# GpSimd's modulation columns in pairs of 256, multiplied by a scalar per partition

## The reference

```python
shift, scale, gate = jnp.split(s_lat @ w_mod[layer] + b_mod[layer], 3, axis=-1)     # first block
x_in = x * (1.0 + scale[:, None, :]) + shift[:, None, :]
...
shift, scale, gate = jnp.split(c_act @ w_ada[l] + b_ada[l], 3, axis=-1)             # second block
h = rms_norm(x, norm_w[l]) * (1.0 + scale[:, None, :]) + shift[:, None, :]
...
x = x + gate[:, None, :] * y
```

## Time and profile before

| | |
|---|---|
| median of three runs | 2867.41 us (2862.24 to 2875.26) |
| span of the profiled execution | 2862.3 us |
| busy: TensorE, VectorE, ScalarE, GpSimd | 95%, 61%, 42%, 52% |
| mean granted TensorE clock | 0.968 |
| loaded from HBM | 589.46 MB |

### The profile page before, as it was taken

How to read it: one execution, slowest core, us unless ns; L and a number is a source line. 1 busy time by engine, 2 the same in 40 slices (tenths; PEclk the granted TensorE clock), 3 DMA queues, 4 the chain that set the end, 5 groups by cost and what they waited for, 6 DMA issues and landing times.

```text
span 2862.3 us, 51222 instructions
## 1 busy us (share of the span) xinstructions
PE 2705.6 (95%) x22151; PEld 2503.6 (87%) x22151; DVE 1738.4 (61%) x1905; ACT 1209.2 (42%) x1438; POOL 1491.9 (52%) x1071
## 2 busy tenths in 40 slices
PE   5799999999999999999999969999989899999899
PEld 3589999888888899989989959999889899998899
DVE  2344545654555658696677655764866557657763
ACT  1243444333443334344476344633453456334442
POOL 0056766986666788777455604054548440445420
PEclk8699999999999999999999979999999999999999
DMA  9999998998887988777556746755657666656565
GB/s 338 290 306 267 267 267 248 293 283 255 244 234 229 282 252 226 207 218 199 144 160 168 206 102 161 187 152 157 185 145 211 192 162 163 170 148 176 154 170 155
DMA packets 948768, 599.21 MB, mean 209 GB/s; under 512 B 22070, under 2 KB 945088, under 8 KB 948032
## 3 DMA queue, kind: packets, MB, share of 16 engines
q1 hardware_dynamic: 944720, 582.83, 72.8%
q10 hardware_dynamic: 3824, 13.11, 1.2%
HBM read 589.46 MB, written 6.29 MB: 208 GB/s over the span
## 4 chain that ended last, share of the span: by engine, by line
PE 78%; DVE 11%; DMA 6%; ACT 3%; issue 1%; SPq 1%; POOL 0%; DVEq 0%; ACTq 0%; POOLq 0%
PE G L2393 58%; DMA ring<-in_w_mod_dram 3%; DVE ring_r L1466 3%; PE A L2333 2%; DMA const<-in_w_mod_dram 2%; PE A L2453 1%; PE A L2459 1%; PE A L2456 1%; PE G L2475 1%; PE A L2494 1%; ACT ring_r L867 1%; PE A L2638 1%; PE G L2831 1%; SPq L718 1%; DVE M L2169 1%
## 5 line engine op out<-in xcount | busy, mean ns | idle before, releaser
L2393 PE MATMUL G<-H_r,ring_r 128*128 128x256 f32 x10032 | 1700.5, 287 | 52.0 <-DVE S_r L1455 20.7
L2393 PEld LDWEIGHTS G<-H_r,ring_r 128*128 128x128 f32 x10032 | 1473.3, 191 | 84.2 <-issue 56.9
L824 POOL TENSOR_TENSOR ring<-ring,act_in 128x512 f32<-128x512 f32 x448 | 659.9, 1494 | 1159.2 <-DMA ring<-in_w_ada_dram 915.9
L1466 DVE TENSOR_TENSOR ring_r<-ring,ring_r 128x2048 fp32r<-128x2048 f32 x346 | 875.1, 2530 | 274.2 <-ACT ring_r L867 273.2
L867 ACT ACTIVATE ring_r<-ring 128x2048 fp32r<-128x2048 f32 x346 | 661.7, 1912 | 334.4 <-PE G L2393 109.9
L2393 PE MATMUL G<-M_r,ring_r 128*128 128x256 f32 x4528 | 789.5, 284 | 0.0
L2393 PEld LDWEIGHTS G<-M_r,ring_r 128*128 128x128 f32 x4528 | 645.5, 190 | 10.0 <-issue 9.4
L2393 PE MATMUL G<-S_r,ring_r 128*128 128x256 f32 x1920 | 546.5, 285 | 0.0
L827 POOL TENSOR_TENSOR ring<-ring 128x512 f32<-128x512 f32 x224 | 366.5, 1636 | 17.6
L2393 PEld LDWEIGHTS G<-S_r,ring_r 128*128 128x128 f32 x1920 | 369.9, 193 | 3.4 <-issue 3.3
L833 POOL TENSOR_TENSOR ring<-ring 128x256 f32<-128x256 f32 x168 | 211.7, 1260 | 13.2
(11 more groups left out here) (441 smaller groups left out, 2581.8 us busy)
## 6 DMA issues: line engine op xcount, KB each, us to landing
ring<-in_w_in_dram SPq DMA_DIRECT2D x120, 1024.0 KB, 5.7
ring<-in_a_w_in_dram SPq DMA_DIRECT2D x98, 1024.0 KB, 6.8
ring<-in_w_ada_dram SPq DMA_DIRECT2D x192, 512.0 KB, 6.8
const<-in_w_mod_dram SPq DMA_DIRECT2D x192, 256.0 KB, 5.4
ring<-in_c_w_in_dram SPq DMA_DIRECT2D x48, 1024.0 KB, 5.9
ring<-in_w_mod_dram SPq DMA_DIRECT2D x16, 2048.0 KB, 18.0
ring<-in_a_w_out_dram SPq DMA_DIRECT2D x32, 1024.0 KB, 6.4
ring<-in_w_out_dram SPq DMA_DIRECT2D x32, 1024.0 KB, 5.9
```

The source lines that it names most:

```text
L824: g.mark(pool.tensor_tensor(w[:, i:i + 2, :], w[:, i:i + 2, :], act_in[:, k:k + 2, c:c + 1].broadcast_to((P, 2, BW)), ALU.mult))
L1466: v.tensor_tensor(w_low(tl), w_raw(tl), w_up(tl).bitcast(F32), ALU.subtract).then_inc(w_lo, 1)
L2393: ins = pe.matmul(G[tl.bank][:, 0:SEQ], w, x, start=(k == 0 and n_ == 0), stop=(k == KT - 1 and n_ == 2))
```

## The change

A block's four units become a pair of blocks' eight units. A unit is now two row groups by 512 columns (still 512 KB; each run of memory that the load reads is 2 KB long, where it was 1 KB). Both blocks of a pair are multiplied and summed together, in rows of 512 columns. The multiply is a `tensor_scalar` with one input and the activation as a scalar per partition. `mod_rows` has two buffers of 512 columns, one for each pair in turn. The columns of both blocks can be transposed only when the pair's last unit is done, and stand at that tile and the next free one. Beside this `ones` and `mean` are stored as one column and read with a broadcast, and `act_in` is stored three columns a row group instead of 32; TensorE's matmuls with `act_in` read 32 consecutive columns, of which the first three are the ones used, as before.

```diff
-    _q = POOL_TILE[4 * _p + 3] - 1
+    _q = POOL_TILE[8 * (_p // 2) + 7] - 1
...
-        ones = sb("ones", [P, P])
-        mean = sb("mean", [P, P])
-        act_in = sb("act_in", [P, KT, 32])
-        mod_rows = [sb(f"mod_rows{i}", [P, BW]) for i in range(2)]
+        one_col, mean_col = sb("one_col", [P, 1]), sb("mean_col", [P, 1])
+        ones, mean = one_col[:, :].broadcast_to((P, P)), mean_col[:, :].broadcast_to((P, P))
+        act_all = sb("act_in", [P, 3 * KT + 32])
+        act_in = act_all[:, 0:3 * KT].rearrange("p (k i) -> p k i", i=3)
+        mod_rows = [sb(f"mod_rows{i}", [P, 2 * BW]) for i in range(2)]
...
-                l, j = POOL_BLOCKS[m // 4]
-                k = 4 * (m % 4)
+                l, j = POOL_BLOCKS[2 * (m // 8)]
+                k = 2 * (m % 8)
...
-                sp.dma_start(pool_unit(m), mod_w[l][:, k:k + 4, j * BW:(j + 1) * BW]).then_inc(pool_full[m % 2], 16)
+                sp.dma_start(pool_unit(m), mod_w[l][:, k:k + 2, j * BW:(j + 2) * BW]).then_inc(pool_full[m % 2], 16)
...
-                for u in range(4):
-                    m = 4 * p + u
+                for u in range(8):
+                    m = 8 * n + u
...
-                    for i in (0, 2):
-                        k = 4 * u + i
-                        g.mark(pool.tensor_tensor(w[:, i:i + 2, :], w[:, i:i + 2, :],
-                                                  act_in[:, k:k + 2, c:c + 1].broadcast_to((P, 2, BW)), ALU.mult))
+                    for i in range(2):
+                        k = 2 * u + i
+                        g.mark(pool.tensor_scalar(w[:, i, :], w[:, i, :], act_in[:, k, c:c + 1], None, ALU.mult))
                     g.settle()
-                    g(pool.tensor_tensor(w[:, 0:2, :], w[:, 0:2, :], w[:, 2:4, :], ALU.add))
                     if u == 0:
-                        if p >= 2:
-                            pool.wait_ge(pool_cols, p - 1)
+                        if n >= 2:
+                            pool.wait_ge(pool_cols, 2 * n - 2)
...
-                    pe.wait_ge(pool_used, 4 * p + 4)
+                    pe.wait_ge(pool_used, 8 * (p // 2) + 8)
...
-                        ins = pe.transpose(bank[:, t * P:(t + 1) * P], mod_rows[p % 2][:, t * P:(t + 1) * P], ident)
+                        c0 = (p % 2) * BW + t * P
+                        ins = pe.transpose(bank[:, t * P:(t + 1) * P], mod_rows[p // 2 % 2][:, c0:c0 + P], ident)
```

More of the change, by code:

```diff
@@ L502, in pool_unit @@
             at = (RAW + HALF) * KT * P + (m % 2) * 4 * BW
-            return ring[:, at:at + 4 * BW].rearrange("p (k c) -> p k c", c=BW)
+            return ring[:, at:at + 4 * BW].rearrange("p (k c) -> p k c", c=2 * BW)
         late = [(CONST_AT["rot128"][0], CONST_AT["keep"][0] + SEQ),
@@ L810, in _ @@
             g = Signals(pool, g_own)
-            for what, value in ((ones[:, :], 1.0), (mean[:, :], 1.0 / D), (act_in[:, :, :], 0.0)):
+            for what, value in ((one_col[:, :], 1.0), (mean_col[:, :], 1.0 / D), (act_all[:, :], 0.0)):
                 g.mark(pool.memset(what, value))
@@ L893, in _ @@
                     act.wait_ge(first_cols, b - 1)
-                act.activation(mod_rows[b % 2][:, :], G[2 * (b % 2)][:, 0:BW], ACT.Copy).then_inc(first_rows, 1)
+                act.activation(mod_rows[b % 2][:, 0:BW], G[2 * (b % 2)][:, 0:BW], ACT.Copy).then_inc(first_rows, 1)
                 if b % 2 and b >= 3:
@@ L2424, in mla @@
                 for j in range(4):
-                    ins = pe.matmul(A[0][:, 0:SEQ], ones[:, :], rms_sq[j], start=(j == 0), stop=(j == 3))
+                    ins = pe.matmul(A[0][:, 0:SEQ], ones, rms_sq[j], start=(j == 0), stop=(j == 3))
                 PS.done(ins, "kvsum")
@@ L2434, in mla @@
                     for j in range(4):
-                        ins = pe.matmul(A[2][:, t:t + 1], rms_sq[j][:, t * P:(t + 1) * P], ones[:, 0:1],
+                        ins = pe.matmul(A[2][:, t:t + 1], rms_sq[j][:, t * P:(t + 1) * P], one_col[:, :],
                                         start=(j == 0), stop=(j == 3))
@@ L2537, in four_sums @@
                 for g in range(4):
-                    ins = pe.matmul(bank[32 * g:32 * g + 32, 0:SEQ], mean[:, 0:32], four[:, g, :], start=first, stop=last,
+                    ins = pe.matmul(bank[32 * g:32 * g + 32, 0:SEQ], mean_col[:, :].broadcast_to((P, 32)), four[:, g, :], start=first, stop=last,
                                     skip_group_check=True)
@@ L2549, in last_sums @@
                     together(bank, part, True, False)
-                return pe.matmul(bank[:, SEQ:2 * SEQ], mean[:, :], x, start=False, stop=(n == KT - 1), skip_group_check=True)
+                return pe.matmul(bank[:, SEQ:2 * SEQ], mean, x, start=False, stop=(n == KT - 1), skip_group_check=True)
             product("ac_out", HR256, HR2, quarters("ac_out"), Pace(sums(0, "ac_out", XH, A[0])))
@@ L2605, in gqa @@
                                 ins = pe.matmul(A[3][:, BW + 4 * t + r:BW + 4 * t + r + 1],
-                                                sq_q1[g % 2][:, r, t * P:(t + 1) * P], ones[:, 0:1], start=True, stop=True)
+                                                sq_q1[g % 2][:, r, t * P:(t + 1) * P], one_col[:, :], start=True, stop=True)
                         PS.done(ins, f"qsum{g}")
@@ L2714, in mixers @@
                                   start=True, stop=True)
-                    pe.matmul(A[2][:, 0:2], ones[:, :], small[:, 50:52], start=True, stop=True)
+                    pe.matmul(A[2][:, 0:2], ones, small[:, 50:52], start=True, stop=True)
                     for p in range(2):
```

10 lines of the change are left out of this document (5 added, 5 removed).

## The result

The changed kernel takes 2842.47 us (median of 4 runs, 2835.71 to 2847.17) against 2864.82 us for the kernel before in 4 runs (2861.77 to 2875.26). The ratio is 0.991, 95% interval 0.9888 to 0.9932. The kernel became faster by about 22 to 26 us (the difference of the medians and the ratio), twice what I forecast, and mostly not by the steps that I forecast.

What follows compares the result with a forecast made beforehand. TensorE, busy 2705.6 of 2862.3 us, was taken as the bound. The terms -3.5 - 7 - 2 + 1.5 = -11 us took the span from 2862.3 to 2851.3 and the median from 2867.4 to 2856.4; 8-in-10 range 2841 to 2876.

Steps and rivals of the forecast that it cites:

- signs I had named: Checks: GpSimd busy near 1190 us; TensorE waiting for VectorE before L2356, or SP for GpSimd above 98.6 us, would refute.
- The duration of the multiply by a scalar: On GpSimd, 512 columns: taken as 0.65 us, near the memset's 0.530, bounded above by 2.1.
- B: VectorE's full stretches: fewer GpSimd pieces block VectorE, and one block's columns leave each norm; -7 us (0 to -15).
- four stretches: From 1100, 1200, 2055 and 2630 us, VectorE nearly full beside GpSimd; TensorE idle 22.1 us together.
- 19 us of waiting in the norms: Two norms, 16 L1672 each, every one losing 0.62 us while GpSimd works.
- only the adds would block, and B would be near -14: If VectorE were free beside one-input instructions, only the adds, 19.4 of 37.5 us, would block it.
- A: SP's 12.6 us hold ending at 2130.37, behind GpSimd's wait for a transpose, goes; -3.5 us (0 to -6).
- C: Stretches at the DMA's limit, 540 to 620 us: longer load runs help a little; -2 us (0 to -6).
- D: Neighbouring transposes: TensorE's second transpose of a pair waits for VectorE's reading of the first; +1.5 us (0 to +6).
- Narrow tensors: Broadcast and 32-column window change only the addresses weight loads read, not the matmuls or columns; 0 us.
- the cheap instruction: Rival, 20%: the one-input multiply takes 0.53 us and VectorE often gets in before GpSimd; -22 us, 2845 us.
- The slow instruction that holds SP: Rival, 10%: from 540 to 620 a slow multiply holds SP's queue and TensorE waits for weights; 2886 us at 1.6 us.

Runs made afterwards that it cites:

- pair_tt: The changed kernel with the two-input multiply of before in place of the multiply by a scalar; 2869.46 us, ratio 1.0018 to the kernel before.
- four_rows: The kernel before with the narrow tensors and four row buffers of 256 columns instead of two; 2858.6 us, ratio 0.9973.
- runs_1k: The changed kernel with each GpSimd unit loaded as two DMAs of 1 KB runs; 2844.5 us, ratio 0.9927 to the kernel before.
- single_ts: The kernel before with narrow tensors and four multiplies by a scalar of 256 columns in each old unit, without pairs; 2906.11 us, ratio 1.0149.
- ports2: Small kernel without the layers' computation, GpSimd and VectorE instructions alone and together; VectorE's 256-column `tensor_scalar` is `a`, 1024-column `tensor_tensor` `b`; memset 524 ns.

## Why the prediction was wrong

The range held the time by 1.5 us (2841 to 2876), and the forecast of -11 us was half of what came. That it came so near is luck: an instruction much slower than I took was priced by a wrong rule, and the two errors went opposite ways. Of the signs I had named, three came against me: GpSimd is busy 1644.8 us and not near 1190, SP waits 113.7 us for it and not below 98.6, and TensorE waits 0.9 us for VectorE before L2356. The steps, one by one.

**The duration of the multiply by a scalar.** Taken 0.65 us, measured 1.57. I bounded it from 0.53 to 2.1 and went to the memset as the nearest row, because one input is less than two. It was the wrong neighbour: the number of inputs does not set the time by itself (a copy, also with one input, takes 614 ns). The scalar column is not what costs, since a multiply by an immediate takes 1490. The Trainium skill (GPSIMD Engine Reference, "When to use GPSIMD") has one-input operations at roughly line rate, from which my estimate was 0.53 to 0.6 us; the trace disagrees with 1.57.

**B, the failed step.** "Only the number of pieces falls": I priced the blocking of VectorE by the mean length of GpSimd's instructions and their number, and held a one-input instruction to block like any other. `pair_tt` has the fewer pieces and loses 5 us; the changed kernel has instructions half as long again and gains 22 to 26. What counts is the form: 0.7 to 0.95 us lost by a scale-and-shift that meets a two-input instruction, 0.2 us beside the multiply by a scalar. From 1.0018 to 0.991 this is 31 us, with an error of 8; less the 7 us that the pair as a unit costs it is 24, against 7 taken and 15 as the far end. The far end was too near because I took it as two thirds of the idle time in four stretches. The 6 us near 1600, the largest single step, lie in none of them: there TensorE waited 5.1 us for VectorE in the kernel before (`PE G L2393 <- DVE X L1685`), and I had left that stretch out of the sum. How the rest is spread over smaller waits is not resolved. The rule of the Trainium skill (SBUF — State Buffer, "SBUF: two separate sides"), on which I leaned, has the pair held exclusively for the whole instruction. By it an `a` beside the 1566 ns multiply would take 1.5 to 1.6 us, an estimate with the two thirds to three quarters of the other's length that it loses beside the two-input ones. It takes 620 ns, so the measurement decides against it for this pair of instructions; for two-input ones the runs are near it. My 19 us of waiting in the norms were a slip, 32 x 0.616 is 19.7, and taken from medians; this changes nothing. The other side I had written down, "only the adds would block, and B would be near -14", was nearer, with a size about half of what came.

**A.** The mechanism was right. The first write of the pair near 2130 starts at once (timeline of the changed kernel, GpSimd; the earlier trace rows has 26.11 us of waiting there):

```profile
2130.94 1.30 POOL L830 TENSOR_TENSOR mod_rows<-ring 128x512 f32<-128x512 f32 x1
```

Its size at the place was 4 to 5 us, near the 3.5 taken. `four_rows` as a whole has 8 us (3 to 12), so whether the buffers bring more than my range of 0 to -6 is open. The other eight waits of SP for a block's first write stayed: 18.6 us in eight before, 17.6 in eight with four buffers.

**C.** Not resolved by `runs_1k`. In the stretch from 540 itself TensorE's idle time fell by 0.2 us. The DMA share there is 1.00.

**D.** Taken +1.5 (0 to +6). The waits before L2356 for VectorE are 0.9 us in the changed kernel, so the mechanism I named is small. The places cost some 6 us (with an error of 6), and the pair as a unit some 7 more that no step of mine had. A coarser hand-over, longer adds and loads in longer runs are what differs; which of these it is I have not separated.

**Narrow tensors.** 0, and nothing was measured (1.0008, 0.9993 to 1.0023).

**The rivals.** The total came out near the cheap instruction's 2845, from an instruction that was the dearest, so that rival was wrong in its mechanism. The slow instruction that holds SP was to decide from t = 1.36: at 1.57 a unit was to take 7.9 us of GpSimd's time against the tile's 7.3. It took 77.3 / 10.8 = 7.1 us (42 instructions, 3.9 a unit), one unit every 7.4. I had scaled GpSimd's waiting with its duration, but it goes by the piece: a multiply waited 0.45 us (mean 1.494 less 1.047) before and 0.56 us (2.125 less 1.569) now, at a length of one and a half. `single_ts` shows the edge from the other side.

The sum as measured, each from ratios times 2864.8 us: -8 for the buffers, +6 for the places, +7 for the pair as a unit, -31 for the multiply by a scalar; -26 in all. The first term has an error of 4, the next two of 6, the last of 8.

## What to carry to other kernels

Where GpSimd works beside a busy VectorE, price its instructions by what they take from VectorE, not by their own length: a one-input form that is half as long again was worth 1% of the whole kernel here. It needs slack on GpSimd, so look first whether the queue that feeds it is held when it gets slower, and make its instructions long before making them slow. Look for the places where TensorE waits behind a row of short VectorE instructions: one such place held some 6 of the 17 us here. And when a trace does not show an instruction, the bound for its interference has to be kept apart from the bound for its duration.

## What the runs showed of the hardware that was not expected

- GpSimd's float32 multiply by a scalar of 512 columns takes 1566 ns, by an immediate 1490, a two-input multiply with a broadcast 1041, one of two full inputs 1262, a copy 614, a memset 524.
- VectorE lengthens GpSimd's instructions by an amount that depends little on their form. Beside an unbroken row of `b` the two-input multiply takes 1620 ns (1041 alone) and the one by a scalar 2253 (1566 alone); beside `a` they take 1057 and 1618 (`ports2`, eight instructions each). The relief of the scalar form goes one way only.
- A memset on GpSimd, which reads nothing, still lengthens VectorE's `tensor_scalar` of 256 columns from 408 to 658 ns, and its `tensor_tensor` of 1024 columns not at all (1219 against 1220).
